# A chain of 25 stages on one core: straight programs of the engines in place of one block per stage, and turns moved into neighbouring stages

## What is computed

```python
for layer in range(DEPTH):                      # 4 layers
    shift, scale, gate = split(silu(c) @ w_mod[layer] + b_mod[layer])   # for x and for ctx
    hx = rmsnorm(x, g_pre[layer]) * (1.0 + scale_x) + shift_x
    yx, yc = mixer(hx, hc, ...)                 # mla, swa, hyena, mla
    x = x + gate_x * rmsnorm(yx, g_post[layer])
    ctx = ctx + gate_c * rmsnorm(yc, g_post[layer])
# mla, swa: attention(h @ w_in) * silu(gate) @ w_out
# hyena:    z = gx[o] * long_conv(z, filt[o]) for two orders, (z * silu(gate)) @ w_out
x = x + hybrid_mixer(rmsnorm(x, g_mix), ...)    # pooling branch and mLSTM heads, merged
x = x + hier_moe(rmsnorm(x, g_ffn), ...)        # 4 groups of 8 experts, top 2
return rmsnorm(x, g_final)
```

## Time and profile before

| what | us |
|---|---|
| median of 3 runs | 2059.43 |
| lowest, highest | 2059.11, 2060.26 |
| the profiled execution | 2061.14 |
| its span in the profile | 2059.4 |
| PE busy | 1905.2 |
| DVE busy | 833.0 |
| ACT busy | 415.3 |

### The profile page before, as it was taken

One profiled execution on the slowest core, in us unless ns is written; L12 is line 12 of the kernel. 1 busy time (PEld: TensorE's weight loads), 2 busy tenths in 40 slices (PEclk: granted clock), 3 DMA queues, 4 the chain that ended last, 5 costly groups with the idle time before them and its releaser, 6 DMA issues. The chain is left out here.

```text
span 2059.4 us, 18886 instructions
## 1 busy us (share of the span) xinstructions
PE 1905.2 (93%) x7154; PEld 1003.7 (49%) x7154; DVE 833.0 (40%) x2073; ACT 415.3 (20%) x1036; POOL 69.0 (3%) x54
## 2 busy tenths in 40 slices
PE   5999999899889899998988999799996999999995
PEld 2545564444554444443344665487864444444442
DVE  4754454673684566524755115343333101100001
ACT  2121242100672222211103223112100111111111
POOL 0000000000000000002420000000000000000000
PEclk8999999999999999999999999899997999999998
DMA  9634101353100344231102231324373999999992
GB/s 373 233 131 165 62 1 36 139 179 121 58 1 0 121 148 157 93 117 41 67 0 82 98 128 42 126 101 167 123 306 114 428 428 427 428 427 428 428 427 83
DMA packets 30376, 362.18 MB, mean 176 GB/s; under 512 B 3499, under 2 KB 3660, under 8 KB 5964
## 3 DMA queue, kind: packets, MB, share of 16 engines
q1 hardware_dynamic: 30284, 360.94, 44.2%
HBM read 359.88 MB, written 1.05 MB: 175 GB/s over the span
## 5 line engine op out<-in xcount | busy, mean ns | idle before, releaser
L696 PE MATMUL bank<-hT,slot 128*128 128x256 f32 (+1 forms) x832 | 266.1, 479 | 0.0
L696 PEld LDWEIGHTS bank<-hT,slot 128*128 128x128 f32 x832 | 157.9, 191 | 101.7 <-issue 90.2
L345 DVE SCALAR_TENSOR_TENSOR product<-slot,cond_rows 128x1024 f32<-128x1024 f32 x160 | 195.6, 1223 | 13.1 <-DMA slot<-panels_dram 4.5
L2426 PE MATMUL bank<-slot,hmT 128*64 128x512 f32 x496 | 174.3, 592 | 1.2 <-ACT hmT L2481 1.2
L1528 PE MATMUL bank<-hT,slot 128*128 128x512 f32 x384 | 170.1, 596 | 1.9 <-PEq L213 1.9
L584 PE MATMUL bank<-slot,gT 128*128 128x512 f32 x384 | 166.7, 593 | 3.8 <-PEq L213 3.8
L2426 PE MATMUL bank<-late_slots,hmT 128*64 128x512 f32 x432 | 139.5, 592 | 0.0
L584 PEld LDWEIGHTS bank<-slot,gT 128*128 128x128 f32 x384 | 72.2, 190 | 92.3 <-issue 92.3
L2522 DVE SCALAR_TENSOR_TENSOR hT<-hT,bank 128x512 f32<-128x512 f32 x16 | 11.0, 688 | 261.5 <-ACT hT L2488 261.5
L1528 PEld LDWEIGHTS bank<-hT,slot 128*128 128x128 f32 x384 | 71.7, 192 | 83.9 <-issue 83.9
L2426 PEld LDWEIGHTS bank<-slot,hmT 128*64 128x64 f32 x496 | 55.4, 137 | 87.6 <-issue 86.2
(11 more groups left out here) (365 smaller groups left out, 2449.0 us busy)
## 6 DMA issues: line engine op xcount, KB each, us to landing
slot<-panels_dram SPq DMA_DIRECT2D x91, 2048.0 KB, 9.7
late_slots<-panels_dram SPq DMA_DIRECT2D x40, 2048.0 KB, 19.6
slot<-panels_dram SPq DMA_DIRECT2D x40, 1024.0 KB, 5.2
branch_slot<-panels_dram SPq DMA_DIRECT2D x9, 2048.0 KB, 22.1
mod_slot<-panels_dram SPq DMA_DIRECT2D x4, 2048.0 KB, 18.5
slot<-panels_dram SPq DMA_DIRECT2D x4, 1536.0 KB, 7.0
slot<-panels_dram SPq DMA_DIRECT2D x2, 1280.0 KB, 20.0
x_tok<-tokens_dram SPq DMA_DIRECT2D x4, 512.0 KB, 10.8
```

Of the source, the lines that this page charges most:

```text
L345: last = m.nc.vector.scalar_tensor_tensor(out=m.product[:], in0=m.slot(panel)[:, c * D:(c + 1) * D], scalar=1.0, in1=m.cond_rows[:, s, :], ...
L696: last = self.m.nc.tensor.matmul(self.bank(g), self.m.slot(panel)[:, k * width + j * P:k * width + (j + 1) * P], self.m.hT[:, k, 0:self.n] ...
L2426: last = nc.tensor.matmul(ps[6 + kind][a * SLOTS:(a + 1) * SLOTS, :], xs[:, k, a * SLOTS:(a + 1) * SLOTS], m.slot(expert_panel(pair, kind, ...
```

## The change

`step()` yields a `Stage`, which writes each engine's piece straight behind its last one: no block, no drain, no barrier and no branch between stages (only the overflow keeps a barrier ahead and a block). In their place stand waits at first uses across stages: `earlier` waits until a signal of a former stage has reached what it had at that stage's end; `hT_ready` and `gT_ready` hold, for each token tile, which counts make it usable, and `tile_of_hT` and `tile_of_gT` wait on them.

With that, work is moved. The last tile's turn of `enter_layer` and `project_out` is kept as `late_turn` and issued in the next stage by `last_tile`: behind the first group in `latent_inputs` and `window_inputs`, behind two half-wide groups in `conv_inputs`, behind two groups in `second_inputs` and ahead of the last tile in `route`. `window_turn` is gone: its 12 batches stand two and two behind the gates 1 to 6 in `window_inputs`, and `qT` has memory of its own. `conv_gate` is gone: `conv_rounds` turns the first half of the channels ahead of its last inverse and the second half at its end. In `latent_qkv` the turns of q stand ahead of the value products. In `second_inputs` the order of the panels and groups changes (the value group first, pooling products behind the first gate).

```diff
     def step(self):
         for s in self.signals.values():
             s.base = s.total
-        with self.nc.Block(no_gpsimd_drain=True) as block:
-            yield block
+        yield Stage(self.nc)
+
+    def earlier(self, eng, *signals):
+        for s in signals:
+            if s.base:
+                eng.wait_ge(s.sem, s.base)
+
+    def tile_of_hT(self, eng, t):
+        for signal, count in self.hT_ready[t]:
+            eng.wait_ge(signal.sem, count)
+
+    def last_tile(self, pe):
+        if self.late_turn is not None:
+            turn, self.late_turn = self.late_turn, None
+            turn(pe)
...
# enter_layer
             columns_to_rows(m, pe, diag, ps[0:4], spread)
-            turn(NT - 1)
+            m.late_turn = lambda pe: turn(pe, NT - 1)
...
# window_inputs, on PE (latent_inputs has the same lines)
+            m.earlier(pe, m.sig("rows_taken"))
             for g, (n, t) in enumerate(groups):
                 i = panels[n]
                 if t == 0:
                     pe.wait_ge(*m.loaded(i))
+                if g == 1:
+                    m.last_tile(pe)
+                m.tile_of_hT(pe, t)
...
                 gates.matmuls(pe, g, i, g % 4)
+                if g == 1:
+                    pe.wait_ge(read.sem, read.at(len(groups)))
+                for c, t in turns_after.get(g, ()):
...
+                        last = nc.tensor.transpose(ps[n % 4][:, b * P:(b + 1) * P], src, m.ident[:, :])
+                    last.then_inc(turned.sem, turned.one())
...
# conv_rounds, on PE
                 if following:
                     filters.products(pe, 1, *following)
                     pe.wait_ge(made.sem, made.at(NX * (r + 1) + 1))
+                else:
+                    turn(0)
                 inverse(r, 1)
+            turn(1)
...
# project_out
-            for t in range(NX):
-                turn(t)
+            turn(pe, 0)
+            m.late_turn = lambda pe: turn(pe, NX - 1)
...
# second_inputs
-        groups = [("if", t) for t in range(NX)] + [(n, j) for n in range(3) for j in range(4)] + [(3, t) for t in range(NX)]
+        groups = [("if", 0), (3, 0), ("if", 1), (3, 1)] + [(n, j) for n in range(3) for j in range(4)]
```

More of the change, by code:

```diff
@@ L677, in _, with __init__ @@
             take_turned(NT - 1)
+        for t in range(NT):
+            m.hT_ready[t] = [(by_dve, by_dve.at(t + 1)), (by_act, by_act.at(t + 1))]
 class Gates:
-    def __init__(self, m, n_tok, tmp, banks=(4, 5, 6, 7)):
+    def __init__(self, m, n_tok, tmp, banks=(4, 5, 6, 7), name="gate"):
         self.m, self.n, self.tmp, self.banks = m, n_tok, tmp, banks
-        self.ready, self.tangent, self.done = m.sig("gate_in_psum"), m.sig("gate_tangent_ready"), m.sig("gate_done")
+        self.ready, self.tangent, self.done = (m.sig(f"{name}_{of}") for of in ("in_psum", "tangent_ready", "done"))
     def bank(self, g):
@@ L1011, in _ @@
                 take_turned(t)
+        for t in range(NX):
+            m.hT_ready[t] = [(by_dve, by_dve.at(t + 1)), (by_act, by_act.at(t + 1))]
 def latent_layer(m, layer):
@@ L1225, in _ @@
                 a += 1
+            pe.wait_ge(d_read.sem, d_read.at(2 * tq))
+            for s, g in turns:
+                pe.wait_ge(d_read.sem, d_read.at(d - 3))
+                for c in range(4):
+                    last = nc.tensor.transpose(ps[4 + d % 4][:, c * P:(c + 1) * P],
+                                               qr[:, s, 4 * g + c].rearrange("p t c -> p (t c)"), m.ident[:, :])
+                last.then_inc(d_ready.sem, d_ready.one())
+                d += 1
             for t in range(NT):
@@ L1274, in _ @@
                     columns.some(dve, 4)
+            for s, g in turns:
+                dve.wait_ge(d_ready.sem, d_ready.at(d + 1))
+                nc.vector.tensor_copy(qrT[:, s, 4 * g:4 * g + 4, :], ps[4 + d % 4][:, :].rearrange("p (c t) -> p c t", c=4)) \
+                    .then_inc(d_read.sem, d_read.one())
+                d += 1
             for t in range(NT):
@@ L1317, in window_inputs @@
         groups = [(n, t) for n in range(3) for t in range(NT)]
+        turned, turned_read = m.sig("qT_in_psum"), m.sig("qT_read")
+        turns = [(c, t) for c in range(4) for t in range(2)] + [(4, t) for t in range(NT)]
+        turns_after = {g: turns[2 * (g - 1):2 * g] for g in range(1, 7)}
         @block.sync
@@ L1515, in _, with channels @@
                 m.load_next(sp, panels[6 + n])
-            sp.wait_ge(filter_units.landed.sem, filter_units.landed.at(64))
         @block.tensor
         def _(pe):
+            def channels(g, tokens):
+                i = panels[g // 4]
+                for k in range(KD):
+                    last = nc.tensor.matmul(ps[g % 2][:, tokens], m.slot(i)[:, k * 512 + g % 4 * P:k * 512 + (g % 4 + 1) * P],
+                                            m.hT[:, k, tokens], start=k == 0, stop=k == KD - 1)
+                return last
+            m.earlier(pe, m.sig("rows_taken"))
+            m.tile_of_hT(pe, NX - 1)
+            pe.wait_ge(*m.loaded(panels[0]))
+            for g in range(2):
+                channels(g, slice(0, N))
+            m.last_tile(pe)
+            m.tile_of_hT(pe, NT - 1)
             for g in range(CH + 1):
@@ L1526, in _ @@
                         pe.wait_ge(conved.sem, conved.at(g - 1))
-                    for k in range(KD):
-                        last = nc.tensor.matmul(ps[g % 2][:, :], m.slot(i)[:, k * 512 + g % 4 * P:k * 512 + (g % 4 + 1) * P],
-                                                m.hT[:, k, :], start=k == 0, stop=k == KD - 1)
-                    last.then_inc(ready.sem, ready.one())
+                    channels(g, slice(N, 2 * N) if g < 2 else slice(0, 2 * N)).then_inc(ready.sem, ready.one())
                 if g in FFN_AT:
@@ L1730, in take, with gate @@
                 nc.vector.tensor_tensor(gate if order == 0 else here, here, gate, ALU.mult).then_inc(gated.sem, gated.one())
+            def gate(half):
+                for t in range(NT):
+                    n = NT * half + t
+                    dve.wait_ge(turned.sem, turned.at(n + 1))
+                    dst = m.gT[:, 4 * half:4 * half + 4, t * P:(t + 1) * P]
+                    back_ = ps[4 + n % 4][:, :].rearrange("p (b t) -> p b t", b=4)
+                    nc.vector.scalar_tensor_tensor(out=dst, in0=back_[:, :, ::-1] if t % 2 else back_, scalar=0.5, in1=dst,
+                                                   op0=ALU.mult, op1=ALU.mult).then_inc(turned_read.sem, turned_read.one())
+            m.earlier(dve, m.sig("gate_done"))
             dve.wait_ge(*m.loaded(filters.decay))
@@ L1750, in _ @@
                     take(r, s)
-            dve.wait_ge(gated.sem, gated.at(2 * R))
+                    if not following and s == 0:
+                        gate(0)
+            gate(1)
         @block.gpsimd
@@ L2027, in _ @@
                     silu(j - 2)
-            dve.wait_ge(spread.sem, spread.at(1))
-            for half in range(2):
-                last = nc.vector.tensor_copy(rbc[:, 2 * half:2 * half + 2, :],
-                                             ps[6 + half][:, :].rearrange("p (h s) -> p h s", h=2))
-            last.then_inc(spread_read.sem, spread_read.one())
             for c in (2 * M_H - 2, 2 * M_H - 1):
@@ L2242, in _ @@
                 nc.vector.tensor_tensor(m.gT[:, c, :], m.gT[:, c, :], gb[:, c, :], ALU.add).then_inc(used.sem, used.one())
+        for t in range(NX):
+            m.gT_ready[t] = used.now()
 def route(m, own, h):
```

289 lines of the change are left out of this document (171 added, 118 removed).

## The result

The changed kernel takes 2015.18 us (median of 4 runs, 2013.72 to 2017.29) against 2059.27 us before (4 runs, 2057.96 to 2060.26): a ratio of 0.9785, 95% interval 0.9773 to 0.9797. That is 44.1 us saved, where 39.4 were forecast; the time lies 4.8 us under the forecast of 2020.0 and inside its range. In the profiled execution the span fell from 2059.4 to 2012.8 us, 46.6 us.

The account below looks back on a forecast made before the run. PE's matmuls were taken as the bound, busy 1905 of 2059.4 us. Savings of 18.7 + 5.8 + 5.5 + 7.8 + 1.6 = 39.4 us from the median 2059.43 gave 2020.0 us, range 2006 to 2034.

Parts of the forecast that it names:

- Plain boundaries (18.7): Stage boundaries where the next work's data is ready: PE restarts without waiting for the barrier, 2.3 + 6.9 + 9.5 = 18.7 us saved.
- First stage (2.3): Start of the kernel: PE starts once ACT has scaled the x tokens, at about 42.7 instead of 45.02, 2.3 us saved.
- Merged turns (11.3): Turning stages merged into their neighbours: 5.8 us saved in the window layer, 5.5 at the convolution layer's end.
- 2.4 us to the first maximum: Window layer: from the gates' end to DVE's first row maximum 2.4 us, plus 5.7 in line, 8.1 instead of 13.9.
- Last tiles (7.8): Last tile's turn moved behind the next stage's first matmuls: 3.05, 3.05, 1.5, +1.0 and -0.8 us, sum 7.8 us saved.
- only from the point at which tile 0 is evicted (L937, to 1326.35): Second block's entry: tile 0's groups fill PE's wait only after that eviction; about 6 us idle remain, +1.0 us gained.
- Filter start (1.6): Convolution's rounds: first filter products no longer wait for the gate's DVE work; their chain starts 1.6 us earlier.
- Convolution's entry (1.5): Convolution layer's entry: no boundary that weighs, only half-width groups ahead of the last tile's turn, 1.5 us saved.
- The first (the clock takes the last tiles' gains back): Rival: the 7.8 us go to 0 and cold stretches stay, saving 27.5 us, time 2032; chance 0.15.
- The second (cold stretches vanish): Rival: low-clock matmuls vanish with the shorter waits, some 11 us more saved, time about 2009; chance 0.14.
- The third: Rival: loads become the bound in the expert stage as it begins earlier, time up to 2065; chance 0.02.
- The fourth (saving under 4 us): Rival: waits at first uses end as late as the barrier did, saving under 4 us, time 2057; chance 0.02.

Follow-up runs that it names:

- the evictions early: Changed kernel with ACT evicting tile 0 and the next gate's rows early, window turns behind the gates: 1987.96 us; last turns at their own stages' ends: 2010.77 us.

## Why the prediction was right, and where it wasn't

**Direction and size: right.** 44.1 us against 39.4. That the two lie so close is luck, for the steps that the runs take apart were off by more and cancelled. Merging with blocks in place gave 4.3 us where the expectations had about 12; leaving the blocks out gave 45.4 where they had 27.5; the deferral cost 5.2 where they had a gain of 4 to 6.

**Plain boundaries (18.7): right in mechanism, too small.** Work that was ready did go on; no load, no queue of DVE was late next. (The two waits of 1.0 us ahead of L584 stand at the first and second layer's end, not at the second and third; the sum is the same.) The first layer gave 11.3 against 9.7, heads and merge 3.0 against 1.5, of which 1.8 was there with blocks too. The step that failed is the price of the low clock: 1.4 us at one place and nothing at most others. One barrier put back costs 9.5 where the forecast had 6.9. With all of them, blocks cost 45.4 us, and 10.4 of the 43.7 in the profile are matmuls at half clock. The 14.0 us by which PE's busy time fell in the changed kernel stand against 1.4, and about 1 for the turn of each last tile, in the sum.

**First stage (2.3): 3.3 in the trace.** PE starts behind ACT's fourth instruction, with a wait of 3.2, as worked out (5.4 before). The 1.1 us that are left of the 3.3 lie ahead of that, where the code is the same, and are within what this row differs by between kernels.

**Merged turns (11.3): the sum right, the reason not.** The window layer saved 9.1 with its layer end where 9.8 were forecast, the convolution's rounds 6.2 where it was 5.5. But with the turns in their former order the window layer saves more, 10.0: what was saved are the boundaries around the turning stages, and the interleaving's part is 0 by the pair of medians (2.0 gained in the convolution, 1.8 lost in the window). The step that failed is "2.4 us to the first maximum": the maximum does come 2.8 us after the first scores' start, but the next wait, for the exponentials, took the gain back.

**Last tiles (7.8): the term with the wrong sign.** By itself the deferral cost 5.2 us. Boundaries behind the last tiles, counted in this term, did go. The waits for the rows were there with 4.0 us as forecast, and a third one at the convolution's entry. At the second block the step that failed is "only from the point at which tile 0 is evicted (L937, to 1326.35)": that row is ACT's half. DVE's half, L968, stands behind the normalisation of tile 1 in DVE's program, and came 3 us later. I had read the eviction of one engine and not of the other. The wait grew from 7.9 to 9.3 us, and dense matmuls at half clock stood behind it. At routing the same row of DVE's (L1035) gave the wait of 5.0.

**Filter start (1.6): right.** From the last gate's end to the first spectrum PE took 6.2 us before and takes 4.6 now.

**Convolution's entry (1.5): 2.2, for another reason.** The stretch of its inputs gave 3.8, of which 1.6 is the filter start. The step that failed is "the convolution layer's entry has no boundary that weighs". The waits of the kernel before have it:

```profile
PE bank L1528 <- PEq L213: 1.9, 1, 1.9
```

It is gone, while the deferral, for which the 1.5 were given, is worth nothing there (305.6 us with it, 305.5 without).

**The rivals.** The first (the clock takes the last tiles' gains back) was true of that term and was outweighed elsewhere. The second (cold stretches vanish) was true of the boundaries, and was the larger. The third did not come: loads stayed ahead of the experts. The fourth (saving under 4 us) is excluded by the result.

## What to carry to other kernels

Ask of each stage boundary what the engine that sets the time could have done meanwhile, and add the half-clock matmuls that the profile shows behind such waits: here they were a quarter of what the barriers cost. Work that is moved into a wait helps only if all its inputs are there when the wait begins; look in the program of each engine that makes them for what stands ahead, since an eviction behind another tile's chain makes the filler into a delay. Measure an edit and its partner together: the deferral cost 5 us alone and was worth 23 with the evictions early.

## What the hardware showed that I had not expected

A barrier of all engines in straight code costs about the same as a block with its branches, 2053.6 against 2055.3 us for 22 of them: the barrier is the cost, not the jump. And with 28 transposes of 128x128 in 3.2 us of a wait of 4 us, the granted clock behind the wait was 1.00 in place of 0.79, at three places worth 4.9 us of the kernel's time; in routing 26 of them gave nothing that shows.
